# TensorE's code for well-filled expert pairs moved behind the program, with a fourth way for up to 64 tokens

## The chip, the cores and the metric

The kernel runs on one core of a Trainium2 chip. Its matrix multiplies run on TensorE (PE in the profile; the loads of its stationary operand are PEld), the element-wise work on VectorE (DVE), the activations on ScalarE (ACT), a little on GpSimd (POOL), and SyncE (SP) issues nearly all DMA transfers. The metric is the device time of one execution in microseconds (us). Each of these engines has a program of its own; they meet only at semaphores.

## The reference

Two blocks of two layers each are computed for 256 tokens of width 1024, all in float32. The first block has four attention branches per layer. The second has one layer of differential attention and one of RWKV-7 time mixing, and behind each of them a mixture of experts (MoE), which is what the change touches:

```python
g_p, g_idx = lax.top_k(g_prob, 1)                    # one of 4 groups
e_p, e_idx = lax.top_k(jax.nn.softmax(e_logits), 2)  # two of its 8 experts
expert = g_idx * 8 + e_idx
...
hg, hu = jnp.split(xb @ w_gu[e], 2, axis=-1)         # 1024 -> 2 x 512
return (jax.nn.silu(hg) * hu) @ w_down[e]            # 512 -> 1024
...
y = y * gate; out = segment_sum(y, tok)              # back to the 256 tokens
```

There are 32 experts, so 512 (token, expert) choices per layer, 16 to an expert on average. How many tokens an expert gets depends on the data. Worked through for the inputs that the reference draws, the first MoE layer has two pairs with an expert over 32 tokens: pair 12 (experts 24 and 25) has 76 and 68, and pair 14 (experts 28 and 29) has 29 and 38. In the second MoE layer only pair 5 (experts 10 and 11, 35 and 15 tokens) is over 32. No expert has over 96.

## The kernel before, in words

Each MoE layer walks over its 16 pairs of experts. SyncE streams the weights: six chunks of 2 MB for a pair (`gu0` to `gu3`, then `dn0` and `dn1`), into a ring of 8 slots (4 `ring` buffers and 4 lent ones in `arena`). A slot is filled again when TensorE has finished with the chunk in it, so SyncE's queue waits on TensorE's semaphore, in the order of the chunks.

A pair is computed in rounds of up to `CAP` = 32 tokens per expert. A round is 32 matmuls with the `gu` weights, four transposes of the result, 16 matmuls with the `dn` weights, and 4 that spread the result back over the 256 tokens. Before the loop VectorE counts the tokens per expert (`behind_oh`) and writes two flags per pair into SBUF: `e.flag`, whether an expert of the pair has over 32 tokens, and `e.flag2`, whether one has over 96. TensorE, VectorE and ScalarE each read the flags into a register (`value_load`) at every pair and branch to one of three pieces of code:

- flag 0, names with `s `: one round;
- flag 1 and flag2 0, names with `m `: three rounds, for which the tokens of rounds 1 and 2 are first gathered by matmuls of `x` with the one-hot table `e.oh2` (in the `lnr` buffer). Rounds 1 and 2 use the buffers `hb`, `cz` and `lnr`;
- flag2 1, names with `f `: all 256 tokens go through both experts.

The code stands in memory in this order for each pair: read the flag and branch, read the second flag and branch, the `f` code, the `m` code, the `s` code. Which code is run has no influence on the number of semaphore steps: each way brings the counts of the three engines to the same value (`mm_to`, `last`, `added`). `next_four` gathers the tokens of the pair after next. The first thing of every way on TensorE are matmuls of the round 0 with `gu0`; in the first pair they wait for ScalarE's copy of the transposed gates (`all in`) and VectorE's `first xe`.

A float32 matmul of the program is two records in the profile, and each record has a weight load of its own; a transpose is one.

## Time and profile before

| what | value |
|---|---|
| time, median of 3 runs | 2185.58 us (2184.54 to 2190.74) |
| the profiled execution's own time | 2183.85 us |
| its span in the profile | 2182.0 us |
| PE busy | 1792.8 us (82%) |
| DVE, ACT busy | 598.6 us, 394.0 us |
| first MoE layer, first matmul with expert weights to last | 888.98 to about 1369.4 us |
| second MoE layer | 1710.03 to about 2166 us |
| DMA over the span | 539.56 MB, mean 247 GB/s |

The program is one long chain of stages. A number such as "PE busy 82%" is a mean over stages with different limits, so the stages have to be looked at one by one: which engine waits, and for what. Idle time that the profile puts down to "issue" is time for which it shows no releaser: the engine's own instruction stream was not there yet, or did something that is no work of the engine (register loads, branches).

### The profile page before, as it was taken

Reading aid. Unit: us, or ns where it says so; the run is one execution under the profiler, and the core shown is the slowest. Engines: PE = TensorE matmul, PEld = TensorE weight load, DVE = VectorE, ACT = ScalarE, POOL = GpSimd, SP = SyncE. Lnnn points to the kernel's source line nnn. Section 1 sums busy time; section 2 is a strip of 40 time slices with the busy share of each in tenths; the row PEclk is TensorE's granted clock in tenths of the full one; section 3 lists DMA queues with packets and bytes.
Section 4 is the critical chain, followed back from the end, with each engine's and each line's share of the span. In section 5 each row is a group of like instructions: output and inputs, shape, how many; then the busy total and the mean of one; then the engine's idle time right before and its main releaser. Section 6 shows DMA issues by size and latency. Waiting matters only on the chain.

```text
span 2182.0 us, 30973 instructions
## 1 busy us (share of the span) xinstructions
PE 1792.8 (82%) x13574; PEld 1121.4 (51%) x13574; DVE 598.6 (27%) x1032; ACT 394.0 (18%) x761; POOL 36.0 (2%) x28
## 2 busy tenths in 40 slices
PE   6999999999999987776676778799987677876654
PEld 4788884879886764322222233565984322322211
DVE  1133312123421145321111121574345221211112
ACT  2323201313301133100000001151222000100001
POOL 0000000000000000000000000001030000000000
PEclk9999999999999998888878999899998788988886
DMA  8322333333243523899999998123004899999995
GB/s 336 99 92 97 135 135 142 146 78 130 83 155 135 212 112 129 369 424 425 424 425 425 426 402 318 66 77 117 4 23 182 375 424 425 418 425 425 426 424 225
DMA packets 51468, 539.56 MB, mean 247 GB/s; under 512 B 7441, under 2 KB 16273, under 8 KB 18225
## 3 DMA queue, kind: packets, MB, share of 16 engines
q1 hardware_dynamic: 49248, 527.06, 59.2%
q0 software_dynamic: 1152, 6.29, 0.8%
q8 instruction: 173, 2.83, 0.5%
q10 hardware_dynamic: 848, 3.00, 0.4%
q14 instruction: 47, 0.38, 0.0%
HBM read 535.28 MB, written 1.05 MB: 246 GB/s over the span
## 4 chain that ended last, share of the span: by engine, by line
PE 68%; DMA 19%; issue 5%; DVE 4%; ACT 3%; DVEq 0%; ACTq 0%
PE ps L410 53%; PE ps L417 13%; DMA arena<-in_moe_w_gu 7%; DMA arena<-in_moe_w_down 7%; DMA ring<-in_moe_w_down 3%; PE ps L423 3%; DMA ring<-in_moe_w_gu 1%; DVE x L1371 1%; ACT arena L2172 1%; DVE arena L1360 1%; ACT hb L2168 1%; DVE mT L1947 0%; ACT arena L2443 0%; DVE mT L1950 0%; ACT L2168 0%
## 5 line engine op out<-in xcount | busy, mean ns | idle before, releaser
L410 PE MATMUL ps<-hT,ring 128*128 128x256 f32 (+2 forms) x1888 | 392.0, 372 | 0.0
L410 PEld LDWEIGHTS ps<-hT,ring 128*128 128x128 f32 (+2 forms) x1888 | 330.5, 184 | 53.8 <-issue 3.4
L417 PE MATMUL ps<-arena 128*32 128x512 f32 (+1 forms) x1572 | 243.5, 706 | 107.5 <-issue 68.1
L417 PE MATMUL ps<-ring,arena 128*32 128x512 f32 x1472 | 211.0, 707 | 99.3 <-issue 73.3
L2172 ACT ACTIVATE arena<-ps 128x512 f32<-128x512 f32 (+4 forms) x145 | 94.5, 652 | 888.5 <-PE ps L417 519.8
L410 PE MATMUL ps<-arena 64*64 64x64 f32 (+10 forms) x1944 | 186.6, 324 | 58.8 <-ACT arena L2443 22.2
L417 PEld LDWEIGHTS ps<-arena 128*32 128x32 f32 (+1 forms) x1572 | 63.9, 130 | 264.0 <-issue 204.8
L1360 DVE TENSOR_TENSOR arena<-arena,ps 128x256 f32<-128x256 f32 (+2 forms) x82 | 46.0, 561 | 551.2 <-ACT arena L2168 464.2
L410 PEld LDWEIGHTS ps<-arena 64*64 64x64 f32 (+4 forms) x1944 | 113.2, 159 | 132.5 <-issue 54.0
L417 PEld LDWEIGHTS ps<-ring,arena 128*32 128x32 f32 x1472 | 53.7, 125 | 238.4 <-issue 196.2
L410 PE MATMUL ps<-ring,hT 128*128 128x256 f32 (+4 forms) x576 | 150.1, 419 | 8.7 <-ACT hT L2168 7.0
L410 PE MATMUL ps<-arena,ring 64*64 64x64 f32 (+2 forms) x1120 | 138.1, 300 | 5.6 <-DVE arena L1371 2.8
L410 PE MATMUL ps<-ring,arena 64*64 64x64 f32 (+3 forms) x1328 | 127.5, 309 | 14.8 <-issue 9.0
L410 PEld LDWEIGHTS ps<-arena,ring 64*64 64x64 f32 (+2 forms) x1120 | 120.8, 163 | 21.0 <-DVE arena L1371 4.7
L410 PEld LDWEIGHTS ps<-ring,hT 128*128 128x128 f32 x576 | 99.4, 192 | 51.7 <-issue 28.7
L410 PEld LDWEIGHTS ps<-ring,arena 64*64 64x64 f32 (+3 forms) x1328 | 71.9, 137 | 62.4 <-issue 55.5
L1947 DVE TENSOR_TENSOR mT<-mT,ps 128x1024 f32<-128x1024 f32 x29 | 35.4, 1221 | 170.8 <-PE ps L410 170.8
L410 PE MATMUL ps<-ring,mT 64*64 64x64 f32 (+1 forms) x704 | 73.3, 286 | 0.0
L423 PEld LDWEIGHTS ps<-tcom,arena 128*128 128x128 f32 (+1 forms) x370 | 41.6, 141 | 61.5 <-issue 57.2
L423 PE MATMUL ps<-tcom,arena 128*128 128x128 f32 (+1 forms) x370 | 52.9, 278 | 24.5 <-ACT arena L2172 24.5
L2168 ACT ACT_TABLE_LOAD x50 | 64.2, 1283 | 44.6 <-DVE small L1365 18.9
L410 PE MATMUL ps<-arena,x 128*128 128x128 f32 x512 | 67.9, 291 | 1.6 <-DVE arena L1360 1.6
(174 smaller groups left out, 1258.8 us busy)
## 6 DMA issues: line engine op xcount, KB each, us to landing
ring<-in_moe_w_gu SPq DMA_DIRECT2D x64, 2048.0 KB, 27.7
arena<-in_moe_w_gu SPq DMA_DIRECT2D x64, 2048.0 KB, 30.9
arena<-in_moe_w_down SPq DMA_DIRECT2D x32, 2048.0 KB, 32.1
ring<-in_moe_w_down SPq DMA_DIRECT2D x32, 2048.0 KB, 31.8
ring<-in_w_merge SPq DMA_DIRECT2D x16, 2048.0 KB, 7.3
ring<-in_w_in SPq DMA_DIRECT2D x10, 2048.0 KB, 7.5
ring<-in_attn_w_qkv SPq DMA_DIRECT2D x6, 2048.0 KB, 7.4
ring<-in_rw_w_rkv SPq DMA_DIRECT2D x6, 2048.0 KB, 7.4
```

Source lines behind the costliest of these rows:

```text
L410: i = t.matmul(o, l, r, start=first, stop=last, skip_group_check=True)
L417: i = t.matmul(o, l, r, start=first, stop=last, skip_group_check=True)
L423: i = t.transpose(o, a, e)
L1360: v.tensor_tensor(o, a, b, op).then_inc(*dve.one(name))
L1371: v.scalar_tensor_tensor(out=o, in0=a, scalar=s, in1=b, op0=op0, op1=op1).then_inc(*dve.one(name))
L1947: v.tensor_tensor(acc[:, 0, :], acc[:, 0, :], psum[1], ADD).then_inc(*added(0, before, pr))
L2168: s.activation(o, a, f, **k).then_inc(*act.one(name))
L2172: s.activation(o, a, ACT.Copy).then_inc(*act.one(name))
```

## The change

TensorE's three ways are now four, and are placed elsewhere. `up_to_cap` (one round) stands in line, behind a compare-and-branch that falls through to it. The others (`several` with R = 2 or 3 rounds, and `any_number`) are written after the end of the second MoE layer by `rare0()` and `rare1()`, for each pair: read a third flag, `e.flag3` (over 64 tokens), go to the two-round code or on; read `e.flag2`, go to the three-round code or to the one for any number; each ends with a branch back to `over`, the next pair's start. On VectorE and ScalarE all ways stay in line, with the two-round way and the reading of `flag3` added inside. VectorE has two more small instructions per MoE layer that compute `flag3`. With two rounds, the third round's matmuls, copies and transposes are left out, and the gathering matmuls of the later tokens move 64 columns in place of 128.

```diff
-    e.flag, e.flag2 = (carve(16).bitcast(mybir.dt.int32) for _ in range(2))
+    e.flag, e.flag2, e.flag3 = (carve(16).bitcast(mybir.dt.int32) for _ in range(3))
@@ tensor_program, moe
+        def several(pr, before, R):
...
+            w2 = 2 * CAP * (R - 1)
+            for half in range(2):
+                mm([(psum[1][:, k * P:k * P + w2], x[:, i, k * P:(k + 1) * P], e.oh2[:, i * P:i * P + w2], i == 0, i == 1)
+                    for k in range(4 * half, 4 * half + 4) for i in range(NT)], N + W + f"tokens{half}")
...
+                if q < 3:
+                    mm_to([o for r in range(1 if q < 2 else 0, R) for o in gu_round(r, q)], before + 8 + q, N + f"gu{q}")
+            for r in range(R):
+                if r < R - 1:
+                    mm(gu_round(r, 3), N + W + f"gu{r}")
+                else:
+                    mm_to(gu_round(r, 3), before + 14, N + "gu3")
...
+        def rare(pr, before, origin):
+            N = M + f"{pr} "
+            with t.bass.body(N + "rare", parent=origin, valid_engines=[t.engine]):
+                more = t.value_load(e.flag3[0:1, pr:pr + 1], min_val=0, max_val=1)
+                t.br_ne(more, 0, N + "more", N + "two")
+                with t.bass.body(N + "two", valid_engines=[t.engine]):
+                    several(pr, before, 2)
+                    t.br(N + "over")
+                with t.bass.body(N + "more", valid_engines=[t.engine]):
+                    most = t.value_load(e.flag2[0:1, pr:pr + 1], min_val=0, max_val=1)
+                    t.br_ne(most, 0, N + "any", N + "three")
+                    with t.bass.body(N + "three", valid_engines=[t.engine]):
+                        several(pr, before, 3)
+                        t.br(N + "over")
...
             many = t.value_load(e.flag[0:1, pr:pr + 1], min_val=0, max_val=1)
-            with t.If(many != 0):
...
+            t.br_ne(many, 0, N + "rare", N + "common")
+            with t.bass.body(N + "common", valid_engines=[t.engine]):
+                up_to_cap(pr, pe.n)
+                t.br(N + "over")
+            t.bass.switch_bb(N + "over")
...
-    moe(0)
+    rare0 = moe(0)
     rwkv()
-    moe(1)
+    rare1 = moe(1)
+
+    rare0()
+    rare1()
@@ vector_program, behind_oh
             ts(cnt2, cnt, 3 * CAP + 0.5, None, ALU.is_gt, None)
             cp(e.flag2, cnt2)
+            ts(cnt2, cnt, 2 * CAP + 0.5, None, ALU.is_gt, None)
+            cp(e.flag3, cnt2)
@@ vector_program and scalar_program, the loop over the pairs
...
+                    more = v.value_load(e.flag3[0:1, pr:pr + 1], min_val=0, max_val=1)
+                    with v.If(more != 0):
+                        several(pr, before, 3)
+                    with v.Else():
+                        several(pr, before, 2)
```

TensorE, around the end of pair 0 and the start of pair 1 of the first MoE layer, in the kernel before. The first two rows end the three-round code, the next six are the one-round code (`arena` and `ring` hold weights, tokens and hidden values), and behind them pair 1 begins:

```order
L417 MATMUL ps<-cz,lnr 128x512 x2
L948 UNCONDITIONAL_BRANCH
L417 MATMUL ps<-ring,arena 32x512 x32
L423 MATMUL ps<-tcom,arena 128x128 x4
L410 MATMUL ps<-arena,x 128x128 x8
L417 MATMUL ps<-arena 32x512 x16
L410 MATMUL ps<-arena 128x512 x2
L417 MATMUL ps<-arena 128x512 x2
L1032 UNCONDITIONAL_BRANCH
L910 TENSOR_LOAD arena
L910 ISA x2
L911 COMPARE_AND_BRANCH
```

TensorE in the changed kernel, from the last transposes ahead of pair 0 to the start of pair 1 of the same layer:

```order
L428 MATMUL ps<-tcom,lnr 128x128 x4
L1100 TENSOR_LOAD arena
L1100 ISA x2
L1101 COMPARE_AND_BRANCH
L422 MATMUL ps<-ring,arena 32x512 x32
L428 MATMUL ps<-tcom,arena 128x128 x4
L415 MATMUL ps<-arena,x 128x128 x8
L422 MATMUL ps<-arena 32x512 x16
L415 MATMUL ps<-arena 128x512 x2
L422 MATMUL ps<-arena 128x512 x2
L1104 UNCONDITIONAL_BRANCH
L1100 TENSOR_LOAD arena
```

The one-round code of pair 0 now follows its compare-and-branch directly; nothing of the other ways lies between two pairs.

TensorE in the kernel before, second half of the three-round code of pair 14, first MoE layer: the `dn` matmuls of rounds 0, 1 and 2 (`arena`, `hb`, `arena` beside the weights in `ring`), twice, and then the return to the tokens (`arena`, then `hb,lnr`, then `cz,lnr` for the third round):

```order
L410 MATMUL ps<-ring,arena 32x512 x8
L410 MATMUL ps<-ring,hb 32x512 x8
L417 MATMUL ps<-ring,arena 32x512 x8
L410 MATMUL ps<-ring,arena 32x512 x8
L410 MATMUL ps<-ring,hb 32x512 x8
L417 MATMUL ps<-ring,arena 32x512 x8
L410 MATMUL ps<-arena 128x512 x2
L410 MATMUL ps<-hb,lnr 128x512 x2
L410 MATMUL ps<-cz,lnr 128x512 x2
L410 MATMUL ps<-arena 128x512 x2
L410 MATMUL ps<-hb,lnr 128x512 x2
L417 MATMUL ps<-cz,lnr 128x512 x2
```

TensorE in the changed kernel, the same half of the two-round code of pair 14, which stands behind the program, and the four rows with which the way to the three-round code goes on:

```order
L415 MATMUL ps<-ring,arena 32x512 x8
L422 MATMUL ps<-ring,hb 32x512 x8
L415 MATMUL ps<-ring,arena 32x512 x8
L422 MATMUL ps<-ring,hb 32x512 x8
L415 MATMUL ps<-arena 128x512 x2
L415 MATMUL ps<-hb,lnr 128x512 x2
L415 MATMUL ps<-arena 128x512 x2
L422 MATMUL ps<-hb,lnr 128x512 x2
L1077 UNCONDITIONAL_BRANCH
L1079 TENSOR_LOAD arena
L1079 ISA x2
L1080 COMPARE_AND_BRANCH
```

One row in three is gone from each piece. A pair with three rounds passes one flag reading and one branch more than before, and steps over the whole two-round code.

## Rows read from the trace of the kernel before

**Rows 1.** The page, part 2: DMA's busy tenths in 40 slices of 54.5 us

```profile
DMA  8322333333243523899999998123004899999995
```

**Rows 2.** The chain that ended last: start us, us, what

```profile
1178.97 36.60 DMA arena<-in_moe_w_down
...
2120.59 38.13 DMA arena<-in_moe_w_down
```

**Rows 3.** Windows of 25 us: busy time per engine, TensorE's granted clock, DMA share, GB/s

```profile
1100.00:1125.00 25.00, 14.29 (x106) 5.30 (x108) 3.27 (x5) 0.98 (x2) 0.00 (x0) 0.84 1.00 425
...
1300.00:1325.00 25.00, 22.45 (x180) 9.26 (x184) 1.12 (x3) 1.36 (x3) 0.00 (x0) 0.86 0.87 359
...
1875.00:1900.00 25.00, 20.36 (x140) 7.88 (x136) 4.20 (x6) 1.58 (x3) 0.00 (x0) 0.86 0.99 411
```

**Rows 4.** Timeline at both MoE starts: start us, us, instruction, [idle before <-releaser]

```profile
881.60 1.27 DVE L1360 TENSOR_TENSOR lnr<-arena 128x128 f32<-128x128 f32 x4
883.69 0.60 PE L423 MATMUL ps<-tcom,lnr 128*128 128x128 f32 x4
884.33 0.60 ACT L2172 ACTIVATE arena<-ps 128x512 f32<-128x512 f32 x1 [1.62 <-PE ps L423]
888.98 1.94 PE L417 MATMUL ps<-ring,arena 128*32 128x512 f32 x8 [4.69 <-issue]
892.41 2.04 SPq L2719 DMA_DIRECT2D ring<-in_moe_w_gu  x2
...
1705.23 0.60 PE L423 MATMUL ps<-tcom,lnr 128*128 128x128 f32 x4
1710.03 2.60 PE L417 MATMUL ps<-ring,arena 128*32 128x512 f32 x16 [4.20 <-issue]
...
1712.67 3.08 SPq L2719 DMA_DIRECT2D ring<-in_moe_w_gu  x2
```

**Rows 5.** Windows of 7 us around both MoE starts, columns as in Rows 3

```profile
886.00:893.00 7.00, 4.02 (x24) 1.17 (x28) 0.44 (x2) 0.00 (x0) 0.00 (x0) 0.76 0.07 21
1707.00:1714.00 7.00, 3.97 (x24) 1.31 (x28) 0.91 (x4) 0.00 (x0) 0.00 (x0) 0.80 0.23 57
```

**Rows 6.** DMA queues from 909 to 911.9 us: queue, packets, MB, share

```profile
q8 instruction: 1, 0.02, 2.2%
```

**Rows 7.** Timeline of PE: first matmuls of pairs 1, 12 and 13

```profile
911.93 3.12 PE L417 MATMUL ps<-arena 128*32 128x512 f32 x13 [4.65 <-issue]
...
1226.32 4.51 PE L410 MATMUL ps<-ring,arena 128*32 128x512 f32 x23 [6.02 <-issue]
...
1232.13 1.48 PE L410 MATMUL ps<-ring,arena 128*32 128x512 f32 x9 [1.30 <-issue]
...
1277.69 2.79 PE L417 MATMUL ps<-arena 128*32 128x512 f32 x12 [3.54 <-issue]
```

**Rows 8.** Timeline of PE through pair 14 of the first MoE layer

```profile
1302.56 6.50 PE L410 MATMUL ps<-arena 128*32 128x512 f32 x32 [6.16 <-issue]
...
1313.19 7.08 PE L417 MATMUL ps<-arena,hb 128*32 128x512 f32 x64
1320.08 1.90 PE L417 MATMUL ps<-arena 128*32 128x512 f32 x16
...
1330.99 1.04 PE L423 MATMUL ps<-tcom,cz 128*128 128x128 f32 x8
1332.77 1.92 PE L410 MATMUL ps<-ring,arena 128*32 128x512 f32 x16 [0.74 <-DVE arena L1360]
...
1345.03 1.02 PE L410 MATMUL ps<-cz,lnr 64*128 64x512 f32 x4
...
1347.60 1.02 PE L417 MATMUL ps<-cz,lnr 64*128 64x512 f32 x4
1352.29 4.05 PE L417 MATMUL ps<-ring,arena 128*32 128x512 f32 x20 [3.67 <-issue]
```

**Rows 9.** Groups of PE by shape: xcount | busy us, mean ns | idle before us

```profile
L410 PE MATMUL ps<-lnr,x 128*128 128x128 f32 x96 | 11.5, 278 | 0.0
...
L410 PE MATMUL ps<-tcom,arena 128*128 128x2 f32 x32 | 4.6, 278 | 0.0
```

More of the change, by code:

```diff
@@ new lines, in any_number @@
+        def any_number(pr, before):
+            N, N0, N1 = M + f"{pr} ", M + f"{pr - 1} ", M + f"{pr + 1} "
+            wg, wd = [N + f"gu{q}" for q in range(4)], [N + f"dn{q}" for q in range(2)]
+            gv, dv = ([wcols(m.w(w), 2, 2 * D) for w in ws] for ws in (wg, wd))
+            pe.n = before
+            t.wait_ge(*dve(N + "all in"))
+            t.wait_ge(*act(N + "all in"))
+            for w in wg:
+                t.wait_ge(*m.w.landed(w))
+            for a in range(2):
+                bufs = (psum[0], psum[1]) if a else (pg, pt)
+                lst = [(dst[:, n * 256:(n + 1) * 256], gv[k // 2][:, k % 2, a * D + c * 512 + n * P:a * D + c * 512 + (n + 1) * P],
+                        hT[:, k, :], k == 0, k == KT - 1)
+                       for c, dst in enumerate(bufs) for n in range(4) for k in range(KT)]
+                if a:
+                    mm_to(lst, before + 14, N + "gu3")
+                else:
+                    mm(lst, N + "f gu0")
+            t.wait_ge(*dve(N + "f hid0"))
+            next_four(pr, pg, N + "f ")
+            for w in wd:
+                t.wait_ge(*m.w.landed(w))
+            t.wait_ge(*dve(N + "f hid1"))
+            for a in range(2):
+                h3 = e.hid[a].rearrange("p (k s) -> p k s", k=4)
+                if a:
+                    t.wait_ge(*act(N1 + "all in"))
+                    t.wait_ge(*dve(N + "f xe"))
+                for i in range(NT):
+                    buf = (pg, pt)[i] if a else psum[i]
+                    lst = [(buf[:, n * 512:(n + 1) * 512], h3[:, k, i * P:(i + 1) * P],
+                            dv[k // 2][:, k % 2, a * D + n * 512:a * D + (n + 1) * 512], k == 0, k == 3)
+                           for n in range(2) for k in range(4)]
+                    if a and i:
+                        mm_to(lst, before + 44, N + "out")
+                    else:
+                        mm(lst, N + f"f down{a}{i}")
+            t.wait_ge(*dve(N1 + "all in"))
@@ new lines, in rare @@
+        def rare(pr, before, origin):
[12 more added lines that the diff above has]
+                        t.br(N + "over")
+                    with t.bass.body(N + "any", valid_engines=[t.engine]):
+                        any_number(pr, before)
+                        t.br(N + "over")
@@ L899, in moe @@
         gates_T(psum[1][:, 0:512], M + "first gatesT")
+        starts = []
         for pr in range(E // 2):
-            N, N0, N1 = M + f"{pr} ", M + f"{pr - 1} ", M + f"{pr + 1} "
-            wg, wd = [N + f"gu{q}" for q in range(4)], [N + f"dn{q}" for q in range(2)]
-            gv, dv = ([wcols(m.w(w), 2, 2 * D) for w in ws] for ws in (wg, wd))
-            before = m.pe.n
+            N = M + f"{pr} "
+            starts.append((pe.n, t.bass.cur_bb))
             if pr == 0:
@@ L1071, in moe, with rest @@
         pe.name(M + "end")
+        def rest():
+            end = pe.n
+            for pr, (before, origin) in enumerate(starts):
+                rare(pr, before, origin)
+            pe.n = end
+        return rest
     def rwkv():
```

383 lines of the change are left out of this document (183 added, 200 removed).

## The prediction, made before the changed kernel had run

> **What bounds the kernel now.** I read the page first: DMA's busy line [rows 1] shows two plateaus at 9, slices 17 to 24 and 32 to 39, and little elsewhere. These are the two MoE layers. The windows say how full the plateaus are: DMA share 1.00 and 425 GB/s in mid-layer, while TensorE is busy for only 14.29 of 25 us [rows 3]. The chain of waits agrees: its longest pieces are waits of 36 to 38 us for a weight chunk [rows 2], and in the second layer the last one ends at 2158.76 us (2120.59 + 38.13), just ahead of the program's end. So in mid-layer TensorE can become faster or slower by several us per pair, and nothing happens. This holds for most of the 32 pair boundaries, at which the change acts.
>
> Two places are different. At the start of a layer SyncE has filled all eight slots and waits for TensorE to empty the first. And at the end of the first layer pair 12 needs three rounds: from 1226.32 us on [rows 7] TensorE is the late one, with DMA down to 0.87 and 359 GB/s at 1300 to 1325 us [rows 3], and pair 14 follows right behind with three more rounds [rows 8]. The second layer's only full pair, 5, lies early; DMA loses little there: 411 GB/s against 425 in one window [rows 3]. That there are three such pairs in all shows in [rows 9]: 96 records of the `lnr,x` gather, 32 to a pair. Which tokens they hold is in the counts of the reference: pair 12 stays at three rounds (76 tokens), pair 14 (38) and pair 5 (35) go to two.
>
> **The price of a branch.** The trace does not show branches, only the idle time around them. At the layers' starts there is one flag reading and one taken branch between the last transposes and the first expert matmul: 4.69 and 4.20 us [rows 4]. Between two one-round pairs there are a branch to the adjacent block, the reading and the taken branch: 4.65 us [rows 7]. So the adjacent branch costs about nothing. Into pair 12 there is one more flag reading and a branch not taken: 6.02 us [rows 7]. Thus reading plus branch not taken L = 6.02 - 4.69 = 1.33 us, and the taken branch J = 4.69 - 1.33 = 3.4 us. What J is made of can be seen: within 909 to 911.9 us, inside the gap of pair 1, one packet of instructions (0.02 MB) is fetched by a queue of its own [rows 6].
>
> The Trainium skill ("Advanced Engine Details and Errata", section Control Flow Timing) gives a branch about 51 ns and a compare-and-branch about 108 ns; by that the 4.7 us would be something that stays, and the layer starts would gain nothing. The Trainium skill also says ("Runtime: NRT & Kernel Launch", section Instruction fetch mechanics) that a taken branch to a target outside the fetched window has to wait for a DMA of its page; by that rule, the trace agrees.
>
> **1. Start of the first layer.** The taken branch becomes a fall-through. After the transposes (end 884.29) TensorE needs L, so 885.6; ScalarE's copy, which the first matmul waits for, ends at 884.93 [rows 4], so it does not hold it. The first matmul comes 3.4 us earlier than 888.98. DMA waits for exactly this: its share is 0.07 from 886 to 893 us [rows 5], and SyncE's next issue is at 892.41, 3.43 us after the first matmul [rows 4]. These 3.43 us are 16 records, which at full pace need 6.89/64 = 0.108 us each [rows 8], 1.8 us with the signal; the clock granted in that window is 0.76, after the idle time [rows 5]. With a shorter idle time some of this comes back; I count half, 0.8 us. Then DMA's pause ends 4.2 us earlier. The whole plateau moves with it, so the gain stays until the end of the layer. **-4.2 us**; bounds 0 and -5.0 (3.4 + 1.6).
>
> VectorE's two extra small instructions for `flag3` lie ahead of the gate tables, which end at 882.87, while TensorE's transposes of them start at 883.69 [rows 4]: 0.8 us of cover for two instructions on 16 columns. Without that cover they would cost their own few tenths. Nothing is counted.
>
> **2. Into pair 12.** Before: 2 L + J, 6.02 us. After: the flag, a taken branch out, `flag3`, a taken branch over the two-round code, `flag2`, fall-through: 3 L + 2 J = 10.7 us. TensorE alone is the path here, and all behind it waits. **+4.7 us**; bounds +1.3 (the second branch free) and +8 (each branch twice as dear behind the program). The idle 1.30 us within the pair's first round, after 23 records [rows 7], looks like the fetch of a following page; whether it returns depends on where the code lies. Left as it is, bound -1.3 to +2.
>
> **3. Out of pairs 12 and 14.** Before, 3.54 and 3.67 us [rows 7, 8], although a branch over the one-round code and a taken one lie there; part of that runs while the last matmuls drain. After: a far branch back, the reading, a fall-through. One branch of each kind against the other: 0, bounds -2 and +2 each. Into pair 14: before 2 L + J, after 2 L + J, since the two-round code stands directly behind its branch: 0. The measured gap is 6.16 us [rows 8].
>
> **4. Pair 14 with two rounds.** It took from 1302.56 to the next gap, 46 us [rows 8]. The third round is 64 records of `gu` and 32 of `dn`, at 0.108 us: 6.9 + 3.45. On the way back 8 records go: four take from 1345.03 to about 1345.89, so 1.7 us [rows 8]. Of the transposes four of the eight `cz` ones and two of the gates' go, and ScalarE no longer copies the third round's result ahead of its first sigmoid, for which TensorE has waited a part of 0.74 us [rows 8]; 0.5 us together. Sum **-12.6 us**. The gather keeps its 32 records at half the columns. Its row has 11.5/96 = 0.12 us per record at 128 columns; the nearest row with few columns, 128x2, has 4.6/32 = 0.14 [rows 9], so narrower is not faster: 0, bound -1.9 (half of 32 x 0.12). The new flag readings on VectorE and ScalarE lie under TensorE's first `gu` round of 6.5 us [rows 8]; without that cover they would cost about L.
>
> Is what TensorE saves its own to keep? The weights of pairs 12 to 15 need 4 x 6 x 2 MB, 118 us at 425 GB/s, after pair 11's last chunk at 1215.6 (1178.97 + 36.60) [rows 2]. So they could be in at 1334 us or a little earlier, and pair 15 starts at about 1340. It just fits.
>
> **5. Second layer.** Start: gap 4.20 - L = 2.9 us, and half of 2.64 - 1.8 us up to SyncE's issue at 1712.67 [rows 4], 0.4: **-3.3 us**, bounds 0 and -3.7; DMA's share is 0.23 in these 7 us [rows 5]. Pair 5 no longer holds the ring: (425 - 411)/425 x 25 us = **-0.8 us**. From there DMA runs at its rate to the last chunk, so whatever the pairs' gaps become, they give nothing.
>
> **Sum:** -4.2 + 4.7 - 12.6 - 3.3 - 0.8 = -16.2 us. Against the profiled execution's own 2183.85 us this is 2167.7. That execution lies 1.7 us under the median of the three runs, and the median is what I forecast: 2185.58 - 16.2 = **2169.4 us**. No change can be told from one of 0.3%, 6.6 us: faster means under 2179.0, slower over 2192.1.
>
> **The rivals.**
>
> A: the gap at the start is not the branch. If the first reading itself costs 4.7 us (TensorE draining, a register load) and a fall-through has it too, the starts give nothing, and pair 12 pays only one L more: +1.3 - 12.6 - 0.8 = -12.1, 2173.5 us. Against it stand the packet [rows 6] and the second reading at only 1.33 us. (The Trainium skill's short branch in Control Flow Timing, above, would lead here.)
>
> B: the branches out of pairs 12 and 14 gain as well, since only one is left of two: 3.6 to 1.3 us twice, 4.5 us, and the stall of 1.3 us vanishes: -22, 2163.6 us. Against it: the way back is as far as the way out.
>
> C: slower, by one mechanism: a branch to code behind the whole program is much dearer than one over neighbouring ways, because its page is never near and DMA is full. On TensorE's path in the tail there are then five far branches (two into 12, one out, one into 14, one out) where there were four at 3.4. With X for one, the sum is 5X - 33 us. The even point is X = 6.6 us; X = 9 gives +12, 2197.6 us. Against it: the branches of before already leave the fetched page, and the next page must come in either case; the distance adds no bytes.
>
> D: DMA takes the gain of the tail. If the last chunks of pair 15 come late, since slots are freed by pair 14 only in its course, the 12.6 us become a wait: about -3.6, 2182.0 us. Against it: DMA has room from 1300 us on [rows 3].
>
> **How the numbers follow.** Forecast 0.62 (its own range 2163 to 2176), A 0.12, B 0.13, D 0.07, C 0.06. The range reaches over A and B, and takes in the bounds of steps 1 to 3: 2161 to 2178; left out are C, D and the tails. Faster (forecast, A, B, less a little) 0.87, within 0.3% 0.08, slower 0.05.
>
> **What would show it.** In the changed kernel's profile: gaps of 1 to 1.6 us in place of 4.7 at each layer's first expert matmul and at most boundaries; DMA's pause there 3 to 4 us shorter; about 10.7 us into the first layer's pair 12, and its body as long as before; pair 14 in 33 to 34 us; no wait for weights in pair 15; the window of pair 5 in the second layer back at 425 GB/s, and its last chunk about 16 us earlier than 2158.76. The forecast is wrong if the fall-through gap stays over 4 us, if a far branch costs much over 3.4 us, or if pair 14's end is followed by a wait for DMA.

## The result, and the profile after

The changed kernel takes **2154.93 us** in the median of 4 runs (2154.29 to 2156.06), against 2185.77 us for the kernel before: ratio 0.9855, 95% interval 0.9838 to 0.9872. That is 30.8 us less, about twice the 16.2 us that were forecast, and under the low end of the range. In the two profiled executions the span falls from 2182.0 to 2153.0 us, by 29.0 us; the sums below are made against that.

DMA's line of the page, to be laid beside [rows 1]: both plateaus begin at 9 where they began at 8.

```profile
DMA  8332333332334432999999999213004999999994
```

The timeline at both starts of the experts' matmuls, beside [rows 4]:

```profile
882.97 0.60 PE L428 MATMUL ps<-tcom,lnr 128*128 128x128 f32 x4
884.25 7.08 PE L422 MATMUL ps<-ring,arena 128*32 128x512 f32 x64 [0.69 <-ACT arena L2237]
886.24 2.04 SPq L2803 DMA_DIRECT2D ring<-in_moe_w_gu  x2
...
1681.73 0.60 PE L428 MATMUL ps<-tcom,lnr 128*128 128x128 f32 x4
1683.02 7.07 PE L422 MATMUL ps<-ring,arena 128*32 128x512 f32 x64 [0.69 <-ACT arena L2237]
1685.00 2.04 SPq L2803 DMA_DIRECT2D ring<-in_moe_w_gu  x2
```

The gap of 4.69 us is one of 0.69, and it is ScalarE's copy that ends it: the flag reading and the branch are hidden. In the second layer 4.20 us become 0.69. SyncE's next issue comes 1.99 us after the first matmul, before it was 3.43. The windows around the starts, beside [rows 5]:

```profile
882.00:889.00 7.00, 6.31 (x60) 2.79 (x61) 2.87 (x8) 0.60 (x1) 0.00 (x0) 1.00 0.77 296
1680.00:1687.00 7.00, 6.31 (x61) 3.38 (x64) 3.57 (x11) 1.20 (x2) 0.00 (x0) 1.00 0.84 324
```

TensorE's granted clock is 1.00 here (its 2.4 GHz), with only 0.69 us of idle time ahead; before, behind gaps of 4.69 and 4.20 us, it was 0.76 and 0.80.

PE's timeline at the pairs' boundaries, beside [rows 7, 8]: pair 0's end, pair 12's start, pair 13's start, pair 14's start, pair 15's start:

```profile
900.09 4.59 PE L422 MATMUL ps<-arena 64*128 64x512 f32 x36
...
1229.80 2.79 PE L415 MATMUL ps<-ring,arena 128*32 128x512 f32 x12 [13.67 <-issue]
...
1275.22 3.64 PE L422 MATMUL ps<-arena 128*32 128x512 f32 x32
...
1298.20 6.57 PE L415 MATMUL ps<-arena 128*32 128x512 f32 x32 [5.92 <-issue]
...
1331.87 2.35 PE L422 MATMUL ps<-ring,arena 128*32 128x512 f32 x20
```

In the first row the last 4 records of pair 0 and the first 32 of pair 1 are one group: there is no gap between them, nor behind pair 12 or 14. At most other boundaries of one-round pairs 0.3 us are left, and the profile ends them with a weight load, not with issue. Into pair 12 there are 13.67 us where there were 6.02, and 10.7 were forecast.

The branches themselves have records, which I had not looked for when I predicted. For each line: count, duration in ns (least, median, most), first and last start in us. First the kernel before, the first flag's branch (L911) and the second flag's (L913, only in the three full pairs):

```profile
L911 PEldq COMPARE_BRANCH  x32: 80/6137/7711, 883.8 to 2133.5; - x32
...
L913 PEldq COMPARE_BRANCH  x3: 6217/6327/6427, 1219.8 to 1829.8; - x3
...
L948 PEldq COMPARE_BRANCH  x3: 313/317/323, 1269.7 to 1878.7; - x3
```

The third row is the branch at the end of the three-round code, over the one-round code to the next pair. Now the changed kernel: the first flag's branch, `flag3`'s, and the return from pair 12 to pair 13:

```profile
L1101 PEldq COMPARE_BRANCH  x32: 63/63/6242, 883.6 to 2104.2; - x32
...
L1074 PEldq COMPARE_BRANCH  x3: 75/75/7160, 1221.7 to 1808.4; - x3
...
L1083 PEldq COMPARE_BRANCH  x1: 306/306/306, 1270.8 to 1270.8; - x1
```

This is the key to the case. A branch that is not taken occupies TensorE's queue for 0.06 to 0.08 us. One taken to instructions that the engine does not hold occupies it for 6.1 to 7.2 us here, and for 5.0 to 7.7 in the kernel before. Some taken branches are cheap: the return to instructions that TensorE left some 55 us earlier takes 0.31 us, and so did the short way forward over the one-round code (L948). The first two kinds were L and J in the prediction, at 1.33 (with the reading) and 3.4 us. "Does not hold" is read from the DMA packets: in the branch ahead of pair 12 (1214.82 to 1220.93 us) a packet of 16 KB of instructions starts at 1218.47, and the branch ends 2.46 us later. (One price lies between: the last pair's branch to the program's end, 3.58 us, for which nothing waits.)

Of the chain that ended last, the two rows that answer to [rows 2], the last chunk of pair 11 in the first layer and the last chunk of the second layer:

```profile
1174.86 36.55 DMA arena<-in_moe_w_down
...
2093.05 37.73 DMA arena<-in_moe_w_down
```

They land at 1211.41 and 2130.78 us, 4.2 and 28 us earlier than before.

### The profile page after: what moved, and what is told of

Same layout as the page of the kernel before. It is cut to its first block, busy times and chain, and to the rows that moved or that the text cites. A ratio compares the mean times of both kernels' runs of the same rounds, so it can differ in the third digit from the quotient of the medians.

```text
span 2153.0 us, 30540 instructions
## 1 busy us (share of the span) xinstructions
PE 1755.8 (82%) x13354; PEld 1090.6 (51%) x13354; DVE 595.3 (28%) x1026; ACT 389.7 (18%) x753; POOL 36.0 (2%) x28
## 4 chain that ended last, share of the span: by engine, by line
PE 61%; DMA 31%; DVE 4%; ACT 2%; issue 2%; DVEq 0%; ACTq 0%
PE ps L415 52%; DMA arena<-in_moe_w_gu 20%; DMA arena<-in_moe_w_down 10%; PE ps L422 7%; PE ps L428 2%; DVE x L1420 1%; ACT arena L2237 1%; DVE arena L1409 1%; ACT hb L2233 1%; DMA ring<-in_w_in 0%; DMA vec<-in_vecs 0%; ACT arena L2233 0%; DVE hT L1432 0%; DVE arena L1424 0%; ACT L2233 0%
## 5 line engine op out<-in xcount | busy, mean ns | idle before, releaser
L422 PE MATMUL ps<-ring,arena 128*32 128x512 f32 x1408 | 192.5, 677 | 102.5 <-DMA ring<-in_moe_w_gu 81.0
L2237 ACT ACTIVATE arena<-ps 128x512 f32<-128x512 f32 (+3 forms) x143 | 93.3, 652 | 856.9 <-PE ps L422 514.9
L422 PEld LDWEIGHTS ps<-arena 128*32 128x32 f32 (+1 forms) x1572 | 55.5, 126 | 273.2 <-DMA arena<-in_moe_w_gu 132.2
L422 PEld LDWEIGHTS ps<-ring,arena 128*32 128x32 f32 x1408 | 42.2, 117 | 235.1 <-DMA ring<-in_moe_w_gu 113.8
L1432 DVE COPY arena<-ps 128x512 f32<-128x512 f32 (+7 forms) x58 | 34.9, 602 | 113.9 <-PE ps L415 108.6
```

Source lines behind the costliest of these rows:

```text
L422: i = t.matmul(o, l, r, start=first, stop=last, skip_group_check=True)
L1432: v.tensor_copy(o, a).then_inc(*dve.one(name))
L2237: s.activation(o, a, ACT.Copy).then_inc(*act.one(name))
```

## The experiments

Twelve kernels ran. "Changed" below is the changed kernel, 2154.9 us and a span of 2153.0.

**1 to 4: where the gain lies.** The first has all four ways in line on TensorE, with no code behind the program:

```diff
-            t.br_ne(many, 0, N + "rare", N + "common")
+            with t.If(many != 0):
+                more = t.value_load(e.flag3[0:1, pr:pr + 1], min_val=0, max_val=1)
...
+                with t.Else():
+                    several(pr, before, 2)
+            with t.Else():
+                up_to_cap(pr, before)
```

> Only the fourth way: all of TensorE's ways stand in line again, in the order any, three, two, one round, so that a one-round pair still branches over the rest; pair 12 reads one flag more, pair 14 takes one branch as before. Branch theory (what the change gained beyond the forecast comes from branches that are gone): only the shorter pair 14 and pair 5 are left, -13.2 and -1 us against the kernel before, 2171 to 2172 us; the gaps of 4.7 us at the layer starts and 3.5 us behind pairs 12 and 14 are back. Rival (the extra gain belongs to the two-round way, because it frees the ring or changes the clock): about 2160 us.

Measured: 2187.85 us, ratio 1.0013 (1.0000 to 1.0026). The fourth way alone gains nothing, and both theories missed, by 16 us and more. Pair 14 is 12.5 us shorter here too (33.6 us against 46.1). PE's timeline behind pair 12, and at pair 15's start, shows where most of it went:

```profile
1283.58 1.08 PE L422 MATMUL ps<-arena 128*32 128x512 f32 x4 [9.76 <-issue]
...
1347.12 1.92 PE L422 MATMUL ps<-ring,arena 128*32 128x512 f32 x4 [5.28 <-issue]
1353.35 5.51 PE L422 MATMUL ps<-ring,arena 128*32 128x512 f32 x26 [4.30 <-issue]
```

The way out of pair 12 now leads over two-round and one-round code and costs 9.76 us against 3.54 [rows 7]; the one out of pair 14 costs 5.28 against 3.67 [rows 8] and is followed by a second gap of 4.30 us. These are 12.1 us. The branch records fit: the one that ends pair 12's code now leads over two ways and takes 6.51 us (L1107) where L948 took 0.31, with 6.80 us for pair 13's own behind it. Another 4.3 us lie in the token-mixing stage (see 9 and 10); they need not belong to the edit.

The second has the code behind the program, but no fourth way: `flag3`'s branch and `several(pr, before, 2)` are left out on all three engines, so that pairs 12, 14 and 5 all take three rounds.

> Only the placement: the ways for over 32 tokens stand behind the program, but there are three of them in all, as before (pairs 12, 14 and 5 take three rounds). Branch theory: the changed kernel plus 13.2 (pair 14) plus 1 (pair 5), less one far branch and reading into pair 12 (7 us), so about 2162 us, with a gap into pair 12 of 6 to 7 us in place of 13.67. Rival (the extra gain belongs to the two-round way): about 2175 us.

Measured: 2155.06 us, ratio 0.9865 (0.9843 to 0.9887), the changed kernel's time, 7 us below the branch theory's 2162 and 20 below the rival's 2175. So the placement alone gives the whole gain. PE's timeline at the starts of pairs 12, 14 and 15:

```profile
1221.28 5.26 PE L415 MATMUL ps<-ring,arena 128*32 128x512 f32 x32 [6.18 <-issue]
...
1289.63 5.22 PE L415 MATMUL ps<-arena 128*32 128x512 f32 x32 [5.56 <-issue]
...
1334.35 3.64 PE L422 MATMUL ps<-ring,arena 128*32 128x512 f32 x32
```

One far branch stands ahead of pair 12, not two: 6.18 us against 13.67. Pair 14 takes 44.7 us with its third round, and pair 15 begins at 1334.35 against 1331.87. So the third round costs 11.1 us in pair 14 and not 13.2. Of the fourth way's 11.1 us, 7.5 are used up by its extra branch and reading; 2.5 are seen at pair 15's start, and the medians do not tell the two kernels apart.

The third was to put a block of instructions between pair 0's branch and its common way:

```diff
+                if pr == 0:
+                    t.br(N + "real")
+                    with t.bass.body(N + "filler", valid_engines=[t.engine]):
+                        any_number(pr, now)
```

> The changed kernel, but in pair 0 of each layer 684 instructions that never run lie between the flag reading and the one-round code, and an unconditional branch steps over them. Branch theory: the first expert matmul comes 4 us (first layer) and 3.5 us (second layer) later, DMA's pause is as long as before, and both stay to the end: +7.5 us, 2162 to 2163 us. Rival (the pause at the start is hidden or given back later): no change, 2155 us.

Measured: 2153.51 us, 0.9862 (0.9843 to 0.9881). No branch leads to the block, and it is not in the program that ran: the gap stays at 0.69 us. It says nothing on the theory, and experiment 7 asks again. But it is a repeat of the changed kernel, 1.4 us from it in the median and 3.1 in the span (2149.9), and shows how far stretches differ with the same code: pair 14 takes 32.2 us in it against 33.7, the way from pair 15's start to the second layer's first expert matmul 346.6 against 351.2, and the rest of the program 473.5 against 470.0.

The fourth makes the way to pair 12's three rounds longer, by `t.br(N + "hop1")` in place of the code, a hop behind pair 13's ways and the code itself behind pair 15's.

> The changed kernel, but on its way to the three-round code pair 12 of the first layer takes two more branches, each to other instructions behind the program (the code stands behind pair 15's, reached over a stop behind pair 13's). Branch theory: 6.2 us each, all on the path, +12.4 us. If the return of the changed kernel was free because the fetched instructions of the next pair were still held (about 8 pages of 16 KB), these two stops push them out, a gap of 2 to 3 us appears behind pair 12, and the time is +15 us, 2170 us. Rival (the return is free because it runs under the last matmuls): no gap behind pair 12, +12.4 us, 2167 us. Second rival (a far branch costs the 3.4 us of the forecast): +7 us.

Measured: 2163.88 us, 0.9913 (0.9893 to 0.9932), 9.0 more than the changed kernel and 10.4 more than its repeat on the same chip. The first hop held no instruction but a branch, and the trace has one more far branch, not two. PE's timeline at the starts of pairs 12 and 13, and the record of the return:

```profile
1233.95 2.79 PE L415 MATMUL ps<-ring,arena 128*32 128x512 f32 x12 [20.30 <-issue]
...
1282.49 3.64 PE L422 MATMUL ps<-arena 128*32 128x512 f32 x32 [2.74 <-issue]
```

```profile
L1126 PEldq COMPARE_BRANCH  x1: 6204/6204/6204, 1275.3 to 1275.3; - x1
```

One more far branch costs 6.63 us ahead of pair 12. And the return, 0.31 us in the changed kernel, is now 6.20: between leaving and coming back 9 packets of instructions were fetched (0.15 MB), before only 6 (0.10 MB). In `pair0_ways_in_line` (7 below) it is 8 packets (0.13 MB), and that return takes 0.33 us. So TensorE keeps more than the block it runs; that the ninth packet pushed out what it left is my reading of this one case. The gap behind is only 2.74 us, since the queue's work begins while the last matmuls still run; this is also why the 6.77 us of the kernel before showed as 3.54 there.

**5 to 7: a shorter way, a hint, and the start.** In the fifth both flags are read in line, and each way has a branch of its own:

```diff
+            more = t.value_load(e.flag3[0:1, pr:pr + 1], min_val=0, max_val=1)
+            t.br_ne(more, 0, N + "more", N + "few")
+            with t.bass.body(N + "few", valid_engines=[t.engine]):
+                t.br_ne(many, 0, N + "two", N + "common")
```

> The changed kernel with both flags read in line and one branch for each rare way (more than 64 tokens: straight to three rounds; 33 to 64: straight to two). Theory (a branch taken to instructions that TensorE does not hold costs 6.2 us of its queue, some 5.9 to 6.2 us of which show): the gap ahead of pair 12 falls from 13.67 to 5.9 to 7 us, all else stays, so 2154.9 - 7 = about 2148 us (2146 to 2150). Rival 1 (the time between the pairs follows where the pages lie, not how many branches there are): the gap stays above 9 us and the time within 2 us of 2154.9. Rival 2 (the second reading and untaken branch in line cost each common pair 0.4 us, 29 pairs): the gap ahead of pair 12 falls, but gaps of 0.3 to 0.5 us appear behind every pair of one round and the time is 2155 or more.

Measured: 2153.92 us (2148.73 to 2156.42), 0.9851 (0.9822 to 0.9880), span 2150.0. The gap ahead of pair 12 is 6.39 us as expected, but only 3 of the 7 us reach the span and the median cannot tell it from the changed kernel. At pair 15's start 5.5 of them are still there (1326.40 us against 1331.87). Of the loss behind it 2.9 us lie in the token-mixing stage (89.8 us against 86.9), which the edit does not touch and which differs as much between kernels whose code there is the same (see 9 and 10). The gaps of 0.30 us behind pairs of one round that rival 2 names are there, but the profile ends them with a weight load (`[0.30 <-DMA ring<-in_moe_w_gu]`), not with issue, and the changed kernel, with one reading, has them too: they do not come from the second reading.

The sixth is this kernel with a prefetch hint ahead of pairs 12, 14 and 5, set in the pair before them (for pair 14 it belongs to the branch to `two`):

```diff
+            if l == 0 and pr in (11, 13) or l == 1 and pr == 4:
+                hints[pr + 1] = t.mark_branch_hint_location()
...
-            t.br_ne(more, 0, N + "more", N + "few")
+            far = t.br_ne(more, 0, N + "more", N + "few")
+            if pr in hints and not (l == 0 and pr == 14):
+                far.branch_hint(hints[pr])
```

> The kernel one_far_branch with a prefetch hint for the branch into the rare way, set by TensorE's queue ahead of the last four matmuls of the pair before, for pairs 12 and 14 of the first layer and pair 5 of the second. Theory (the 6.2 us are the fetch of instructions, so a fetch that starts earlier shortens them): the hint stands some 1 to 3 us ahead of the branch in the queue, so the gaps ahead of pairs 12 and 14 fall by 1 to 3 us each, or to nothing where the queue runs further ahead: 2136 to 2146 us. Rival (the hint is not heeded, or its fetch pushes out what comes next and is followed by a second one): gaps of 6 us and more, 2148 us or slower.

Measured: 2152.54 us, 0.9839 (0.9805 to 0.9873), the time without the hints. Records of the hints and of pair 12's branch:

```profile
L1062 PEldq BRANCH_PREFETCH_HINT  x3: 41/46/55, 1213.7 to 1799.9; - x3
...
L1105 PEldq COMPARE_BRANCH  x32: 63/66/6108, 885.9 to 2108.0; - x32
```

The hint runs at 1213.7 us, 3.9 us ahead of the branch at 1217.7, and the branch still takes 6.11 us. Between 1213 and 1219.8 us no packet of instructions moves; the one for the branch starts at 1221.27. The hinted branches of pairs 14 and 5 take 6.17 and 7.46 us. In this form the hint did nothing. Why is open.

The seventh is the changed kernel with the rare ways of pair 0 alone back in line ahead of its common way:

```diff
             t.br_ne(many, 0, N + "rare", N + "common")
+            if pr == 0:
+                n = pe.n
+                rare(pr, n, starts[0][1])
+                pe.n = n
```

> The changed kernel with the rare ways of pair 0 alone (both layers) back in line ahead of its common way, which is now reached by a taken branch over them. Theory (the whole gap of 4.69 and 4.20 us at the start of the experts was this branch): the gap at the first expert matmul returns, 4 to 5.3 us in both layers, the weights' loads start 4 to 6 us later in both, and since the loads pace both stages nearly all of it reaches the end: 2155 + 7 to 9 = 2162 to 2164 us. Rival (the start gain in the changed kernel came from elsewhere, or the loads' lead is lost later): the gap returns but the time is within 2 us of the changed kernel's, 2153 to 2157.

Measured: 2171.39 us (2167.79 to 2173.55), 0.9939 (0.9920 to 0.9958). The start's gain is gone, and more than that: 16 us, where 7 to 9 were expected. PE's timeline and a window of pair 0, and behind it the same window of the changed kernel:

```profile
888.05 9.01 PE L422 MATMUL ps<-ring,arena 128*32 128x512 f32 x64 [4.77 <-issue]
...
888.05:895.05 7.00, 7.00 (x51) 1.81 (x55) 0.00 (x0) 0.00 (x0) 0.00 (x0) 0.80 0.35 110
```

```profile
884.25:891.25 7.00, 7.00 (x64) 1.99 (x64) 1.36 (x5) 0.00 (x0) 0.00 (x0) 1.00 0.80 307
```

Behind 4.77 us of idle time the 64 records take 9.01 us at a mean clock of 0.80, against 7.08 at 1.00. The branch costs 4.1 us as a gap and another 1.9 as a slower clock; 4.3 us of the 6.0 are left at the layer's end. In the second layer the gap is 4.07 us, the way from the reading to the first matmul 4.5 us longer, and pair 0 takes 2.3 us longer. With 3.2 us between the layers, and 1.3 lost again, these are the 13.0 us by which the span grew. The 3.2 us are a net figure: the token-mixing stage between the layers is longer by 6.8 us, and these need not belong to the edit (see 9 and 10). One piece of them is a gap of 4.03 us put down to issue, where the changed kernel has none:

```profile
1475.80 2.89 PE L415 MATMUL ps<-arena 64*64 64x64 f32 x178
1482.72 2.41 PE L415 MATMUL ps<-arena 64*64 64x64 f32 x78 [4.03 <-issue]
```

**8 to 10: one reading, and where straight code lies.** In the eighth VectorE writes 0, 1 or 2 into `e.flag`, and TensorE reads once: `t.br_eq(many, 2, N + "more", N + "few")`, then `t.br_ne(many, 0, N + "two", N + "common")`.

> The kernel one_far_branch with one reading instead of two: VectorE writes 0, 1 or 2 into the one flag (0: up to 32 tokens; 1: up to 64; 2: more), and TensorE compares the one register with 2 and then with 0. Theory (in one_far_branch the second reading of 0.3 us, with 0.15 us behind it, was no longer covered by the last matmuls and showed as 0.3 us at about half of the pairs): the gaps of 0.30 us behind pairs of one round go to nothing, the gap ahead of pair 12 stays at 6.4 us, and the profiled execution is 2 to 3 us shorter than one_far_branch's 2150.0 us of span, the median at 2149 to 2152 us. Rival (those 0.30 us were the untaken branch's or are made up for by the weights' loads): the same time as one_far_branch, 2152 to 2156.

Measured: 2152.77 us (2149.99 to 2157.29), 0.9854 (0.9829 to 0.9878), span 2150.0, as in experiment 5: the rival's time. It is so partly by chance, for PE's timeline of pair 12 shows a gap that nobody had asked for:

```profile
1222.52 1.92 PE L415 MATMUL ps<-ring,arena 128*32 128x512 f32 x4 [5.91 <-issue]
1227.68 6.46 PE L415 MATMUL ps<-ring,arena 128*32 128x512 f32 x28 [3.23 <-issue]
```

The way's first 4 records run, and then TensorE stands for another 3.23 us. With the slower clock behind it pair 12 takes 52.1 us where it took 45.8 in experiment 5, and stretches that no edit touched give this back: from pair 15's start to the second layer's first expert matmul it is 347.7 us against 352.0. So the equal times do not show that the second reading is free. What speaks for it is that the gaps of 0.30 us are still there with one reading (`[0.32 <-DMA ring<-in_moe_w_gu]`), as in the changed kernel.

The ninth and tenth are the changed kernel with its code from pair 8 of the first layer on placed by `t.addr_align(256, offset=0, max_nops=0)`, or 128 (slots of 64 bytes; 256 of them are one packet of instructions).

> The changed kernel, its instructions as they are, but with TensorE's code from pair 8 of the first layer on placed at slot 0 of a 16 KB instruction block (one branch over padding, within a wait for weights). Theory (TensorE stalls where its straight code runs out of fetched instructions, and where these stalls fall depends on how the code lies against the 16 KB blocks): the stretch from GpSimd's third mark to its fifth in the token-mixing stage, 86.8 us in the changed kernel (89.0 before, 93.3 in two_rounds_in_line, 93.7 in pair0_ways_in_line), differs by more than 2 us between aligned_0 and aligned_128, and the total time with it by 2 to 7 us. Rival (these differences come from the memory or are of the profile): both stretches lie within 1 us of 86.8 and both times within 2 us of 2155.

> As aligned_0, with the same code placed at slot 128 of a 16 KB block. Theory: a different time from aligned_0 by 2 to 7 us, most of it in the token-mixing stage, with stalls of TensorE that the trace puts down to issue at other places. Rival: the same time as aligned_0 within 2 us.

Measured: 2158.61 us (2158.0 to 2161.4) and 2161.82 (2156.92 to 2163.53), ratios 0.9880 and 0.9885. Both lie above the changed kernel. Their medians differ by 3.2 us, but the single runs overlap, and the stretch between GpSimd's marks (additions at 1475.5 and 1562.3 us in the changed kernel) is 91.0 and 91.5 us in them, not 2 us apart: neither the theory nor its rival holds. That this stretch hangs on where the main code lies alone fell with the kernels 8, 11 and 12: their main code is the same, and it took 86.6, 88.5 and 90.4 us. In all of them it has gaps of 1 to 4 us put down to issue among thousands of 64x64 matmuls, those of 0.9 us and more make 2.8 us in sum in the changed kernel and 9.8 in `pair0_ways_in_line`. What sets their length is open.

**11 and 12: where the rare ways lie.** Only the places of the three ways that the data takes differ, by an alignment ahead of the branch that ends the block before each:

```diff
+                    if l == 0 and pr == 12:
+                        t.addr_align(256, offset=255, max_nops=0)
                     t.br(N + "over")
...
+                        if (l, pr) in ((0, 13), (1, 4)):
+                            t.addr_align(256, offset=255, max_nops=0)
                         t.br(N + "over")
```

> The kernel one_flag_far_branch with the three rare ways that this data takes (three rounds of pair 12 and two of pair 14 in the first layer, two of pair 5 in the second) placed so that each begins at slot 0 of a 16 KB instruction block; no other instruction changes. Theory (a far branch costs the fetch of the block that it lands in, 6.2 us of the queue, and a further 3.2 us where the landing place is so near the block's end that the next block is not there yet, as in one_flag_far_branch ahead of pair 12 behind 4 matmuls and ahead of pair 5 behind 9): the second gap of 3.23 us within pair 12 goes, the gaps ahead of pairs 12 and 14 stay at 5.5 to 6.4 us, span 2146 to 2148 us against 2150.0 (the gap at pair 5 goes too, but the weights' loads cover that one). Rival (the second gap comes of something else, the data or the clock): it stays, span and time as in one_flag_far_branch, 2150 and 2153.

> As ways_at_slot_0, but the three ways begin at slot 236, 20 instructions ahead of a block's end. Theory: all three show a second gap of 2.5 to 3.5 us behind the first few matmuls, pair 14 too, which had none in one_flag_far_branch: 6 to 7 us longer than ways_at_slot_0 (span 2152 to 2155). Rival: the same time as ways_at_slot_0 within 2 us, and no second gap ahead of pair 14.

Measured: **2147.11 us** (2146.91 to 2147.25), ratio 0.9826 (0.9811 to 0.9841), and 2158.59 us (2157.33 to 2161.5), 0.9877 (0.9858 to 0.9895). The theory held for the gaps (pair 5 has its second one at slot 236 too, 3.04 us); the difference of the medians is 11.5 us where 6 to 7 were expected. At slot 0, pairs 12 and 14 start so:

```profile
1221.65 5.43 PE L415 MATMUL ps<-ring,arena 128*32 128x512 f32 x32 [5.72 <-DVE lnr L1413]
...
1289.43 5.68 PE L415 MATMUL ps<-arena 128*32 128x512 f32 x32 [4.81 <-DVE lnr L1413]
```

At slot 236 both have a second gap. Behind the timeline stand windows of pair 12, for the clock: two at slot 236 and, last, one at slot 0.

```profile
1222.70 1.93 PE L415 MATMUL ps<-ring,arena 128*32 128x512 f32 x7 [6.04 <-issue]
1227.86 4.96 PE L415 MATMUL ps<-ring,arena 128*32 128x512 f32 x25 [3.22 <-issue]
...
1295.22 2.74 PE L415 MATMUL ps<-arena 128*32 128x512 f32 x9 [4.86 <-DVE lnr L1413]
1300.63 5.35 PE L415 MATMUL ps<-arena 128*32 128x512 f32 x23 [2.67 <-issue]
```

```profile
1222.70:1227.80 5.10, 1.93 (x7) 0.20 (x8) 0.00 (x0) 0.00 (x0) 0.00 (x0) 0.50 1.01 424
1227.80:1233.80 6.00, 5.94 (x34) 2.32 (x34) 0.00 (x0) 0.00 (x0) 0.00 (x0) 0.69 1.01 426
```

```profile
1221.60:1227.60 6.00, 5.95 (x37) 2.01 (x38) 0.00 (x0) 0.00 (x0) 0.00 (x0) 0.69 0.98 415
```

From the end of the pair before to the end of the first 32 records pair 12 needs 11.15 us at slot 0 (1215.93 to 1227.08) and 16.15 at slot 236 (1216.67 to 1232.82), and pair 14 5.1 us more in the same way: 10.1 of the 14.6 us between the two profiled executions. The second gap is 3.22 and 2.67 of them. Most of the rest is the clock: after the first gap it is at 0.50 (1.2 GHz) up to the end of the second gap, and then as low (0.69) as it is at slot 0 behind the first.

The packets show what the second gap waits for. At slot 236 the next packet of instructions starts at 1225.41 us, 10.1 us after pair 12's branch, and TensorE goes on 2.45 us later; at slot 0 it starts just as late, 9.8 us after the branch, but there TensorE has a whole block of 256 instructions to run first. Pair 14 at slot 236 goes on 2.4 us after its packet too, and so does pair 12 after its stall of 1.30 us in the kernel before [rows 7].

`ways_at_slot_0` is the fastest kernel of this study, 7.8 us under the changed one. (The releaser "DVE lnr" in its rows had been done for long; the branch record in the gap is 6.05 us.)

## Why the prediction was wrong, point by point

The forecast was -16.2 us, the profiled executions differ by -29.0. Piece by piece:

- **Step 1, start of the first layer: -4.2 forecast, -4.2 measured.** The last chunk of pair 11 lands at 1211.41 against 1215.57 us. That the number was hit is partly luck: the gap shrinks by 4.00 us and not by 3.4, since the reading is hidden, the transposes ahead of it end 0.72 us earlier anyway (883.57 against 884.29), and SyncE's issue comes 6.17 us earlier (892.41 to 886.24), since the clock stays at 1.00. Of this 2 us are lost again by the last chunk of pair 11.
- **Step 2, into pair 12: +4.7 forecast, +7.7 measured** (13.67 against 6.02). This is the step in which J was mis-sized: 3.4 us from the visible gap, where the branch records say 6.11 for the first one and 7.16 for the second, in which two packets were fetched. Two things went wrong. J was the gap less L, and L = 1.33 was the difference of two gaps that each held one taken branch: on record these are 5.03 us at the layer's start and 6.33 into pair 12, and their difference is nearly all of L. The reading itself takes 0.31 us, and 0.8 us pass from one branch to the next with it; at the start all of it lay under the matmuls. And a gap shows only what of the branch sticks out behind the matmuls that still run; 0.5 us lay under them in these two, 1.3 in pair 1. The second branch of a chain has no such cover and costs its whole 6.2 us and more, as `two_more_hops` (+6.63) and `placed_only` (-7.5) confirm. The upper bound of +8 held.
- **Step 3, out of pairs 12 and 14: 0 forecast, -3.54 and -3.67 measured.** This is the largest miss in sign. "One branch of each kind against the other" counted a branch as one price. The forecast set the far way back equal to a taken branch of J. It costs 0.31 us and is hidden, as the branch over the one-round code was before (L948); what is gone is pair 13's and pair 15's own taken branch over the rare ways, into code that was not fetched yet (6.77 and 6.91 us in the queue). Rival B had this at 0.13, with 4.5 us for both, and the argument against it, "the way back is as far as the way out", was false: it is as far, and costs a twentieth. What counts seems to be whether the block is still held; in `two_more_hops`, with 9 packets in between, the same return costs 6.20 us.
- **Inside pair 12: a stall left as it was, -2.4 measured.** The 1.30 us [rows 7] went, the rest I take for the clock. Experiments 11 and 12 show that such a stall belongs to the landing place: 3 us at slot 236, none at slot 0. Where the ways of the kernel before and the changed one lie was not chosen, so these 2.4 us are luck.
- **Between pair 13's start and pair 14's: not in the forecast, -1.9.** Of this 1.6 us are pair 13's own time. The clock is 1.00 in its first 6 us, without a gap ahead; in the kernel before it was 0.72, behind 3.54 us. The other kernels agree: with no gap ahead this stretch takes 17.1 us in nearly all of them, and behind 9.76 us (`two_rounds_in_line`) 18.4; before it took 18.7. (A gap of 2.74 us in `two_more_hops` cost nothing here: 17.1.)
- **Step 4, pair 14 with two rounds: -12.6 forecast, -12.4 measured** (46.1 us to 33.7, gap left out), and DMA did not take it (rival D). The term is right (the repeat in experiment 3 has 32.2 us, with a higher clock at its start), but the kernel pays for it: with its own added branch and reading (7.5 us in pair 12), and `placed_only` without both is as fast. What the fourth way is worth when its branch is not in the path of pair 12 no pair of runs shows by itself: `one_far_branch` (2153.9) cannot be told from `placed_only` (2155.1), and `ways_at_slot_0` has the landing places changed as well.
- **Between the layers: 0 forecast, -3.1.** The same instructions. From pair 15's start to the second layer's first expert matmul the changed kernel and its repeat differ by 4.6 us, so I do not put it down to the change.
- **Step 5, second layer: start -3.3 forecast, -3.5 measured; pair 5 -0.8 forecast, -1.0; the end another -1.0.** Only the start is clear of chance: behind it the layer takes 470.0 us in the changed kernel, 472.0 before, and 473.5 in the repeat.

Two readings in the prediction are slightly off and change nothing in it: 2120.59 + 38.13 is 2158.72 and not 2158.76, and slices 17 and 32 of DMA's line stand at 8, not at 9.

The sum: -4.2 + 7.7 - 7.2 - 2.4 - 1.9 - 12.4 - 3.1 - 3.5 - 1.0 - 1.0 = -29.0 us. Against the forecast that is +3.0 for step 2, -7.2 for step 3, -4.3 for stall and clock in pairs 12 and 13, -3.1 between the layers, and -1.2 for the small rest. Rival A (the gap at the start is no branch) is refuted by `pair0_ways_in_line`: the gap comes back at 4.77 and 4.07 us. Rival C put the even point at 6.6 us for one far branch; they did cost 6.1 to 7.2, yet the kernel is faster. C counted the returns as far branches, and took the four of the kernel before at 3.4 us: on record those are 6.33, 6.77, 6.43 and 6.91, against three of 6.11, 7.16 and 6.24 now.

In short, the step that failed is the price of a taken branch: J as one price of 3.4 us for the way in and the way back. The runs showed 6.1 to 7.2 us on the way in and 0.31 us back. The two errors have opposite signs; step 3 and the shorter stall and higher clock behind it outweighed step 2.

The Trainium skill ("Runtime: NRT & Kernel Launch", section Instruction fetch mechanics) says that a taken branch outside the fetched window waits for a DMA of its page; the trace agrees, with 6.1 to 7.2 us. The same section of the Trainium skill says in one place that the instruction memory is only two lines of 16 KiB; the return of 0.31 us after 6 fetched packets does not agree with that, and the measurement decides. In another place that section of the Trainium skill gives TensorE's as 128 KiB, which are eight such blocks, and the returns after up to 8 packets (0.33 us) and after 9 (6.20 us) agree with that. The 51 and 108 ns of the Trainium skill ("Advanced Engine Details and Errata", section Control Flow Timing) are of the size of the branches not taken here, 63 to 88 ns; those taken into code that is not held cost some sixty times as much.

## What to carry to other kernels

Put the common way of a branch in line behind it and the rare ones behind the program, and give each rare way one far branch from the main path, not a chain: in a chain every link after the first costs its whole time, since no matmul runs above it. Look at the branch records of the engine's queue and not only at the idle time around them, and let the landing place lie at the start of an instruction block. And count the clock with the gap: an idle time of 4.8 us cost TensorE another 1.9 us in the matmuls behind it.

## What the runs showed of the hardware that I had not expected

- A branch taken to instructions that TensorE does not hold: mostly 5.9 to 7.2 us of its queue (4.6 to 7.7 in all), whether the target stood behind the neighbouring ways or behind the whole program. A packet of instructions starts some 3.6 us after the branch in most of them, and the branch ends about 2.5 us later. Not taken: 0.06 to 0.09 us. Taken back to instructions left up to 8 packets before: about 0.3 us, at most 0.43; 9 packets before, in one run: 6.20 us.
- Landing 20 instructions ahead of a block's end costs a second stall of 2.7 to 3.2 us, and 5 us with the clock; two such landings made 10.1 us of difference between kernels with the same instructions.
- A prefetch hint 3.9 us ahead of the branch led to no earlier packet.
- In line, a second flag's reading (0.31 us, with 0.15 behind it) and an untaken branch added no gap that the profile puts down to issue: they ran under the pair's last matmul records, which take about 2 us.
- Between executions of the same code the time between the two expert stages differed by 4.6 us, and TensorE's part of it has gaps of 1 to 4 us put down to issue whose cause is open.
